# Sampled rows' input projection of the gated DeltaNet layer: column halves side by side, three weight slots, output rows ahead of the scan's loads

## What is computed

```
def _dn_branch(xn, S0, conv_buf, w_in, conv_w, A_log, dt_bias, o_gain, w_out):
    qkv, z, b, a = _split(xn @ w_in, (3072, 1024, 8, 8))
    qkv, new_buf = _short_conv(qkv, conv_buf, conv_w)      # silu of a 4-tap convolution; new_buf: last 3 rows of each request
    ...                                                    # q, k normed; delta rule over chunks of rows
    beta = sigmoid(b)
    g = -exp(A_log) * softplus(a + dt_bias)
    o, S_new = _gated_delta_chunked(q, k, v, g, beta, S0)
    return (_rms_norm(o, o_gain) * silu(z)) @ w_out, S_new, new_buf
```

## Time and profile before

| what | value |
|---|---|
| median of three runs | 2249.23 us (2243.47 to 2261.52) |
| the profiled execution's own time | 2251.16 us |
| its span, first to last instruction | 2248.6 us |
| around the span | 2.6 us |
| TensorE busy, mean granted clock | 90% of the span, 0.948 |
| `dn_sample`, from its first TensorE transpose to the scan's first | 1686.4 to 1763.1 us, 76.7 us |

### The profile page before, as it was taken

One profiled execution on the slowest core, in us unless ns is written; L12 is line 12 of the kernel. 1 busy time (PEld: TensorE's weight loads), 2 busy tenths in 40 slices (PEclk: granted clock), 3 DMA queues, 4 the chain that ended last, 5 costly groups with the idle time before them and its releaser, 6 DMA issues. The chain is left out here.

```text
span 2248.6 us, 25250 instructions
## 1 busy us (share of the span) xinstructions
PE 2030.2 (90%) x9247; PEld 1230.7 (55%) x9247; DVE 1380.2 (61%) x2311; ACT 674.4 (30%) x1699; POOL 502.5 (22%) x544
## 2 busy tenths in 40 slices
PE   6999999998788989788899978989999799999998
PEld 5544344443455566444444545656543687767774
DVE  2478678999678999388683212122332576666662
ACT  3447622121324233111012221112111444443431
POOL 2112100000000000011105666664401512322220
PEclk9999999999999999898999988889999899999999
DMA  4025420110521120212123434343458352233210
GB/s 132 12 77 203 138 87 24 47 47 24 196 78 55 38 85 22 75 42 72 51 56 104 125 113 122 106 120 101 136 189 289 90 180 79 65 82 79 74 45 29
DMA packets 158113, 207.32 MB, mean 92 GB/s; under 512 B 43968, under 2 KB 107768, under 8 KB 157944
## 3 DMA queue, kind: packets, MB, share of 16 engines
q1 hardware_dynamic: 135016, 152.87, 21.1%
q0 software_dynamic: 16896, 50.35, 7.0%
q10 hardware_dynamic: 6080, 2.49, 0.4%
HBM read 161.94 MB, written 43.74 MB: 91 GB/s over the span
## 5 line engine op out<-in xcount | busy, mean ns | idle before, releaser
L1837 PE MATMUL acc_ch<-xnT,w_ch 128*128 128x512 f32 x736 | 367.0, 650 | 5.4 <-ACT x_pad L1870 5.4
L1837 PEld LDWEIGHTS acc_ch<-xnT,w_ch 128*128 128x128 f32 x736 | 147.2, 209 | 168.2 <-issue 163.9
L857 PE MATMUL acc<-w_qg,xnT 128*128 128x512 f32 x384 | 173.5, 606 | 11.5 <-DVE sgate L1011 11.5
L1727 POOL DMA_INDIRECT kg<-in_cache_k,rowidx x128 | 128.2, 1002 | 178.5 <-DVE rowidx L1994 78.4
L1734 POOL DMA_INDIRECT home<-in_cache_v,rowidx x128 | 131.5, 1027 | 64.8 <-issue 31.7
L1052 DVE MAX8 top_v<-scores 128x8 f32<-128x4100 f32 x32 | 141.7, 4430 | 0.7
L1054 DVE FIND_INDEX8 top_i<-top_v,scores 128x8 uint32<-128x4100 f32 x32 | 141.5, 4423 | 0.0
L1056 DVE MATCH_REPLACE8 scores<-top_v,scores 128x4100 f32<-128x4100 f32 x32 | 141.2, 4414 | 0.0
L2799 PE MATMUL PB<-home,ogT_dn 128*128 128x512 f32 x288 | 129.1, 602 | 11.4 <-DVE rhs L3063 10.6
L857 PEld LDWEIGHTS acc<-w_qg,xnT 128*128 128x128 f32 x384 | 72.6, 194 | 96.4 <-issue 84.1
L1233 PE MATMUL ring<-w_out_att,ogT_blk 128*128 128x512 f32 x256 | 114.5, 606 | 4.4 <-DMA w_out_att<-in_att_w_out 2.9
(11 more groups left out here) (437 smaller groups left out, 3719.5 us busy)
## 6 DMA issues: line engine op xcount, KB each, us to landing
home<-in_dn_w_in SPq DMA_DIRECT2D x7, 2048.0 KB, 8.2
w_ch<-in_dn_w_in SPq DMA_DIRECT2D x24, 512.0 KB
qkv_d<-y_ch SPq DMA_DIRECT2D x24, 512.0 KB
qkv_t<-qkv_d SPq DMA_DIRECT2D x8, 1536.0 KB, 7.9
x<-in_x_all SPq DMA_DIRECT2D x9, 512.0 KB, 3.4
out_y_all<-y_t SPq DMA_DIRECT2D x9, 512.0 KB, 2.7
w_z_s<-in_dn_w_in SPq DMA_DIRECT2D x1, 4160.0 KB
w_kvq<-in_att_w_in SPq DMA_DIRECT2D x2, 2048.0 KB, 8.0
```

What stands on the lines that cost most here:

```text
L857: ins = pe.matmul(acc[rows(n), k % ACC, :], xnT[:, kk, cols(n)], w[:, kk, :], start=(kk == 0), stop=(kk == KT - 1))
L1727: pool.indirect_dma_start(kg[:, j % KR, :], None, ck, bass.IndirectOffsetOnAxis(ap=rowidx[:, u % 2, t * QT + u // 2:t * QT + u // 2 + 1], ...
L1837: ins = pe.matmul(acc[:, s, :], w[:, c % WR, k, :], xT[:, k, s * 512:(s + 1) * 512], start=(k == 0), stop=(k == KT - 1))
```

## The change

It touches `dn_sample` alone.

- `project` puts the two halves of 256 columns of a piece side by side: half h goes to output partitions 64h to 64h+63 of the same PSUM bank, two matmuls of 256 columns in place of one of 512 for each k. `gates` does so with the two halves of z (512 columns each). b and a have a load (`w_ba`, 128 x 8 runs of 64 bytes) and matmuls (`steps`) of their own.
- A piece is then 128 partitions x 256 columns: `row` takes it with all 128 partitions (the row scales are copied to partitions 64 to 127 by one more VectorE instruction), and `turn` needs two transposes of 128 x 128 in place of four of 64 x 128. tanh of z is one instruction of 128 x 512 and moves behind the Ln.
- Weight pieces have three slots (`home` twice and `w_more`). Piece 2 is issued at once, piece n from 3 after the matmuls of piece n - 3.
- The old convolution rows have a tile of their own (`cb_n`), so that their load waits for nothing, and their transposes come after the second piece.
- In the queue `wz` comes after the weight pieces, and the stores of the new convolution rows (16 of them now, each 3 rows x 6 runs of 1 KB) come after the constants and ahead of the scan's tile, states, `gz_t1` and `y_t1`.

```
 @block.sync
+            def load(u):
+                if u >= WS:
+                    sp.wait_ge(mm, u - WS + 1)
+                sp.dma_start(w[u % WS], wv[:, :, u * 512:(u + 1) * 512]).then_inc(w_in[u % WS], 16)
-            sp.wait_ge(ss_ok, 1)
             sp.dma_start(cb_n, ...)
+            load(2)
             ...
-            sp.dma_start(wz[:], wv[:, :, CONV:CONV + 1040]).then_inc(wz_in, 16)
-            for n in range(2, CONV // 512):
-                sp.wait_ge(mm, n - 1)
-                sp.dma_start(w[:, n % 2, :, :], wv[:, :, n * 512:(n + 1) * 512]).then_inc(w_in[n % 2], 16)
+            sp.dma_start(w_ba[:], wv[:, :, CONV + DM:CONV + DM + 16]).then_inc(wb_in, 16)
+            for u in range(3, NR):
+                load(u)
+            sp.dma_start(wz[:], wv[:, :, CONV:CONV + DM]).then_inc(wz_in, 16)
             ...                                            # eight constants
+            sp.wait_ge(row_ok, NR)
+            for b in range(DB):
+                for h in range(2):
+                    t = h * NS + (b + 1) * DS
+                    sp.dma_start(d["newbuf_s"][b * 3:(b + 1) * 3, :].rearrange("i (n h j) -> h i n j", h=2, j=HW)[h],
+                                 nat[t - 3:t, :].rearrange("i (n j) -> i n j", j=HW)).then_inc(nb_out, 16)
             sp.dma_start(keep["qkv_t1"][:], ...)
             ...                                            # states, gz_t1, y_t1
-            sp.wait_ge(row_ok, NR)
-            for b in range(DB):
-                sp.dma_start(d["newbuf_s"][b * 3:(b + 1) * 3, :], nat[(b + 1) * DS - 3:(b + 1) * DS, :]).then_inc(nb_out, 16)
-            sp.wait_ge(nb_out, 16 * DB)
+            sp.wait_ge(nb_out, 32 * DB)

 @block.tensor, project(u)
-                    ins = pe.matmul(acc[0:NS, u % 2, :], xT[:, k, :], w[:, u % 2, k, :], start=(k == 0), stop=(k == KT - 1))
+                    for h in range(2):
+                        ins = pe.matmul(acc[h * NS:(h + 1) * NS, u % 2, 0:HW], xT[:, k, :], w[u % WS][:, k, h * HW:(h + 1) * HW],
+                                        start=(k == 0), stop=(k == KT - 1))
 @block.tensor, turn(u)
-                for c in range(4 * u, 4 * u + 4):
-                    ins = pe.transpose(cbp[:, u // 2 % 2, (c % CG) * NS:(c % CG + 1) * NS], nat[:, c * P:(c + 1) * P], ident[0:NS, 0:NS])
+                for i in range(2):
+                    ins = pe.transpose(dst[:, i], nat[:, u * HW + i * P:u * HW + (i + 1) * P], ident[:])
 @block.tensor, gates()
+                    for h in range(2):
+                        ins = pe.matmul(yp[h * NS:(h + 1) * NS, 0, :], xT[:, k, :], wz[:, k, h * 512:(h + 1) * 512], start=(k == 0), stop=(k == KT - 1))
 @block.tensor, order
             for u in range(NR):
                 project(u)
+                if u == 1:
+                    buffers()
                 if u >= 1:
                     turn(u - 1)
-            gates(2)
+            steps()
             turn(NR - 1)
-            gates(0)
-            gates(1)
+            gates()
 @block.scalar
-            for c in range(2):
-                act.wait_ge(z_done, c + 2)
-                act.activation(th[0:NS, c * 512:(c + 1) * 512], yp[0:NS, c, :], ACT.Tanh, scale=rsh[:]).then_inc(th_ok, 1)
             act.wait_ge(ach, 1)
             act.activation(t2[:], t2[:], ACT.Ln, bias=1.0).then_inc(ga, 1)
+            act.wait_ge(z_done, 2)
+            act.activation(th2[:], yp[:, 0, :], ACT.Tanh, scale=rsh[:]).then_inc(th_ok, 1)
 @block.vector
+            dve.tensor_copy(rs[NS:, :], rs[0:NS, :]).then_inc(rs_ok, 1)
```

More of the change, by code:

```diff
@@ L2113, in dn_sample @@
     NR = CONV // 512
-    CH = [(CONV, 512), (CONV + 512, 512), (CONV + 1024, 16)]
     with ExitStack() as ctx:
@@ L2120, in sem @@
             return new_sem(nc, env, "sm_" + name)
-        wz = sb("w_z_s", [P, KT, 1040])
-        w = keep["home"][:].rearrange("p (a k n) -> p a k n", a=2, k=KT)
+        HW = 256
+        WS = 3
+        wz = sb("w_z_s", [P, KT, DM])
+        w_ba = sb("w_ba_s", [P, KT, 16])
+        w_more = sb("w_more_s", [P, KT, 512])
+        home = keep["home"][:].rearrange("p (a k n) -> p a k n", a=2, k=KT)
+        w = [home[:, 0], home[:, 1], w_more[:]]
         x, th = keep["y_t0"], keep["gz_t0"]
+        th2 = sb("tanh_pair", [P, 512])
         go = sb("gain_o_s", [NS, HD])
@@ L2127, in dn_sample @@
         ss = sb("ss_s", [NS, 1])
-        rs = sb("rs_s", [NS, 1])
+        rs = sb("rs_s", [P, 1])
         mhalf = sb("mhalf_s", [NS, 1])
@@ L2138, in dn_sample @@
         thc = sb("tanh_s", [P, NCH, NS])
-        nat = sb("rows_s", [NS, CONV])
-        cb_n, junk = nat[0:NB3, :], nat[:, 0:DM]
+        nat = sb("rows_s", [P, NR * HW])
+        cb_n = sb("conv_buf_s", [NB3, CONV])
+        junk = th[0:NS, :]
         yp = keep["acc_ch"]
@@ L2148, in dn_sample @@
         once = sem("once")
-        wz_in, cb_in = sem("wz_in"), sem("cb_in")
-        w_in = [env["stores"]["ws_in0"], env["stores"]["ws_in1"]]
-        rsh = sb("rs_half_s", [NS, 1])
+        wz_in, cb_in, wb_in = sem("wz_in"), sem("cb_in"), sem("wb_in")
+        w_in = [env["stores"]["ws_in0"], env["stores"]["ws_in1"], sem("ws_in2")]
+        rsh = sb("rs_half_s", [P, 1])
         ss_ok, rs_ok, go_ok, tp_done, xT_ok = (sem(s) for s in ("ss_ok", "rs_ok", "go_ok", "tp_done", "xT_ok"))
@@ L2162, in _ @@
         def _(sp):
-            sp.wait_ge(ss_ok, 1)
-            sp.dma_start(cb_n, d["state_dn_conv"].rearrange("b l i n -> (b l i) n")).then_inc(cb_in, 16)
+            def load(u):
+                if u >= WS:
+                    sp.wait_ge(mm, u - WS + 1)
+                sp.dma_start(w[u % WS], wv[:, :, u * 512:(u + 1) * 512]).then_inc(w_in[u % WS], 16)
+            sp.dma_start(cb_n[:], d["state_dn_conv"].rearrange("b l i n -> (b l i) n")).then_inc(cb_in, 16)
+            load(2)
             sp.dma_start(go[:], d["dn_o_gain"][0:1, :].partition_broadcast(NS)).then_inc(once, 16)
@@ L2195, in _ @@
             link(pool.tensor_scalar(ss[:], ss[:], 1.0 / DM, EPS, ALU.mult, ALU.add))
-            pool.tensor_tensor(rs[:], ss[:], mhalf[:], ALU.pow).then_inc(rs_ok, 1)
-            pool.wait_ge(rs_ok, 1)
+            pool.tensor_tensor(rs[0:NS, :], ss[:], mhalf[:], ALU.pow).then_inc(rs_ok, 1)
+            pool.wait_ge(rs_ok, 2)
             pool.tensor_scalar(rsh[:], rs[:], 0.5, None, ALU.mult).then_inc(rs_ok, 1)
@@ L2217, in _, with buffers @@
             ins.then_inc(tp_done, 1)
[L2218 to L2222, removed]
+            def buffers():
+                pe.wait_ge(cb_in, 16)
+                for c in range(NCH):
+                    ins = pe.transpose(cbp[:, c // 16, (c % 16) * NB3:(c % 16 + 1) * NB3], cb_n[:, c * P:(c + 1) * P], ident[0:NB3, 0:NB3])
+                ins.then_inc(cb_done, 1)
             def project(u):
-                pe.wait_ge(w_in[u % 2], 16 * (u // 2 + 1))
+                pe.wait_ge(w_in[u % WS], 16 * (u // WS + 1))
                 if u >= 2:
@@ L2236, in turn, with steps, gates @@
                     pe.wait_ge(x_ok, 1)
-                for c in range(4 * u, 4 * u + 4):
-                    ins = pe.transpose(cbp[:, u // 2 % 2, (c % CG) * NS:(c % CG + 1) * NS], nat[:, c * P:(c + 1) * P], ident[0:NS, 0:NS])
+                dst = cbp[:, u // 2 % 2, u % 2 * 256:(u % 2 + 1) * 256].rearrange("p (h i t) -> p i h t", h=2, i=2)
+                for i in range(2):
+                    ins = pe.transpose(dst[:, i], nat[:, u * HW + i * P:u * HW + (i + 1) * P], ident[:])
                 if u % 2 == 1:
                     ins.then_inc(tr_done, 1)
[L2242 to L2246, removed]
+            def steps():
+                pe.wait_ge(wb_in, 16)
                 for k in range(KT):
-                    ins = pe.matmul(dst, xT[:, k, :], wz[:, k, a - CONV:a - CONV + n], start=(k == 0), stop=(k == KT - 1))
+                    ins = pe.matmul(bps[0:NS, 0:16], xT[:, k, :], w_ba[:, k, :], start=(k == 0), stop=(k == KT - 1))
                 ins.then_inc(z_done, 1)
+            def gates():
+                pe.wait_ge(wz_in, 16)
+                for k in range(KT):
+                    for h in range(2):
+                        ins = pe.matmul(yp[h * NS:(h + 1) * NS, 0, :], xT[:, k, :], wz[:, k, h * 512:(h + 1) * 512], start=(k == 0), stop=(k == KT - 1))
+                ins.then_inc(z_done, 1)
+            pe.wait_ge(xT_ok, 1)
             for u in range(NR):
                 project(u)
+                if u == 1:
+                    buffers()
                 if u >= 1:
                     turn(u - 1)
-            gates(2)
+            steps()
             turn(NR - 1)
-            gates(0)
-            gates(1)
+            gates()
         @block.scalar
@@ L2261, in _, with buffers @@
             act.activation(junk, x[0:NS, :], ACT.Square, accum_out=ss[:]).then_inc(ss_ok, 1)
[L2262 to L2267, removed]
+            act.wait_ge(rs_ok, 3)
+            def buffers():
+                act.wait_ge(cb_done, 1)
+                for u in range(2):
```

(17 more changed lines are left out.)

## The result

| | before | changed |
|---|---|---|
| median, us | 2250.82 (20 runs) | 2238.73 (20 runs, 2226.13 to 2245.31) |
| ratio of changed to before | | 0.9941, 95% interval [0.9924, 0.9959] |
| span of the profiled execution | 2248.6 | 2231.5 |
| `dn_sample`, first transpose to the scan's first | 1686.41 to 1763.06: 76.65 | 1680.06 to 1746.10: 66.04 |
| from there to the span's end | 485.5 | 485.4 |

12.1 us faster by the medians; by the ratio it is 0.6%. The prediction had 14.7. In the stage itself the gain is 10.6 us; behind it nothing came or went. So I compare stage lengths from here on: identical code gave 66.0 and 66.2.

The account below looks back on a forecast made before the run. A loop of load and matmuls bounds the stage's first half, DMA bytes the second. Terms 28.7 + 10.3 + 10.3 + 4.1 = 53.4 us start the scan 14.7 us earlier: 2249.2 - 14.7 = 2234.5 us, range 2221 to 2249.

Parts of the forecast that it names:

- The block ends with the DMA queue: End of `dn_sample`: SyncE is through issuing at 1747.9, the scan starts at 1748.4 in place of 1763.06.
- The rival in which the queue doesn't hold the block: Issues of states and `gz_t1` return early, z's path ends the block: 26 us less, 2223 us; chance 0.10.
- Pairs: Weight pieces in `project`: paired matmuls of 256 columns overlap, 0.215 us a pair, 3.4 us a piece.
- no overlap: Pairs of 256 columns don't overlap, the last piece ends about 1736: gain 2 us, 2247 us; chance 0.05.
- a low clock: TensorE's clock stays low, pieces take 6.9 us: gain 2 at worst, 8 in the middle, 2241 us; chance 0.08.
- Start of the stream: Weight queue in `dn_sample`: piece 0 ends at 1694.4, piece 3 is issued at 1694.5; b's and a's load costs 0.
- The output rows' price: Stores of new convolution rows: 4.1 us on three engines; their 5.4 us of issues lie beside z's load.
- The sum: From piece 3's issue to the end of `y_t1`'s issue: 28.7, 10.3, 10.3 and 4.1, together 53.4 us.
- output rows nearly free: Stores of new convolution rows cost 0.7 us, spread over all engines: 18.1 us less, 2231 us; chance 0.12.
- The slower rival: Scan's loads queue behind 288 store runs on three engines; priced by runs these cost 49 us: 2280 us; chance 0.03.
- z's path: z's weights land at 1723.2, matmuls take 9.5 us, all done at 1736.6, 11 us before SyncE is through.
- Loads behind the stores: Part of the slower rival, chance 0.03: the scan's loads, 4 MB of states included, queue behind the stores' 288 runs.

Follow-up runs that it names:

- run 6: Changed kernel with the loads of both state halves, `gz_t1` and `y_t1` moved to the scan's queue: stage 52.2 us against 66.04, ratio to before 0.9900.
- run 5: Changed kernel with the two halves of z's matmuls one after the other instead of in pairs: stage 66.2 us against 66.04.
- run 1: Changed kernel with the two halves of a weight piece one after the other instead of in pairs: stage 78.3 us against 66.04.
- run 4: Changed kernel with each of the 16 stores split in two, 3 rows x 3 runs: stage 64.1 us against 66.04.
- run 10: Kernel before the change with its eight stores moved ahead of the scan's loads: stage 82.6 us against 76.65.
- run 9: Changed kernel with two weight slots instead of three: stage 74.6 us against 66.04.
- run 2: Changed kernel with its 16 stores put back behind the scan's loads: stage 73.1 us against 66.04.
- run 8: Kernel before the change with the loads of both state halves, `gz_t1` and `y_t1` moved to the scan's queue: stage 75.8 us against 76.65, ratio 0.9983.

## Why the prediction was right, and what was off

- *The block ends with the DMA queue, after the change with the issues of states and `gz_t1`.* Right, and shown by run 6 (13.8 us when these alone are moved) and run 5 (nothing when TensorE is slowed at the end). The rival in which the queue doesn't hold the block falls.
- *Pairs.* 3.67 us a piece for 3.4; they overlap at 256 columns, and the clock was 1.00 from 1690 to 1705.5, so the rivals of no overlap and of a low clock fall too. Run 1 shows what the pairs are worth here: 12 us, and only by releasing the stores and the scan's loads.
- *Start of the stream.* Piece 3 was issued 7.97 us into the stage, forecast 8.1. But what I wrote beside it, that b's and a's runs of 64 bytes are free because the queue waits for piece 0 anyway, was wrong in kind: the stretch 1688 to 1690 runs at 190 GB/s and a share of 1.04, at piece 3's issue, so the DMA engines were not waiting. Two us at 190 in place of some 385 GB/s are about 1 us of the stream. In runs 5 and 6 piece 3 was issued 0.4 us earlier and the last constant's issue came no earlier for it (32.2 us into the stage each time). That the 64-byte runs are the cause is argued from these rows; a run without the load wasn't made.
- *The output rows' price* is the step that was mis-sized. The prediction let the issues of the 16 stores (0.34 us each, 5.4 in all) lie beside z's load and charged only 4.1 us of bytes on three engines. The bytes were sized well (68 GB/s in run 4 for the 72 assumed), but a store took SyncE 0.78 us from one issue to the next, 12.5 in all. Of these 6.5 lay behind the last of the weights and constants, and the data of the scan's tile began to move 1.5 us after the last of them: together the hole of 8 us. So it is SyncE's issuing that costs and not the three engines. The sign that the prediction named for this, a share of 0.17 for much over 4 us, is there.
- *The sum.* The stream, 53.4 us from piece 3's issue to the end of `y_t1`'s, was 57.6. Of the 4.2 between them 1.3 lie ahead of z's landing (30.0 us after piece 3's issue, where the sum has 28.7), the 64-byte runs most likely; 2.9 lie behind it, where the hole was 3.9 longer than the term and about 1 was made up, which I have not traced. That the gain in the stage is 10.6, to the digit that of the upper bound of 8.2 us for the stores, is therefore luck.
- *The other prices of the rows.* The rival "output rows nearly free" falls. The slower rival had the right kind of price for part of it, by the run and not by the byte, with a chance of 0.03. It put it on the three engines, where the runs of run 4 passed at 68 GB/s, about 45 ns each on an engine; SyncE's issues come to 12.5 us, where 18.8 would have decided against the change.
- *z's path.* Forecast 50.2 us into the stage (1736.6), measured 50.6, by two misses that cancel: the weights landed 1.1 us later, and the matmuls took 8.48 us in place of 9.5.
- *Loads behind the stores.* This part of the slower rival is real: in the kernel before it costs 6 us (run 10), in the changed one it is what makes run 1 slower than before. What kept it from deciding is that the last piece ends 31 us into the stage, where it was 54 before.

So the parts depend on each other: three slots (8.6 us, run 9), pairs (12, run 1) and the order of the queue (7, run 2) are each worth two thirds of the gain of 10.6 or more, their sum is far more than the gain, and run 10 shows one of them alone as a loss.

## What to carry to other kernels

Where a block ends with a DMA queue, ask what the queue's own engine must still issue. Behind other transfers each of the states' and `gz_t1`'s loads held SyncE for 3.5 to 8.0 us, and loads that nobody in this block needs were better issued at the head of the next one (14 us here, more than any single part of the change is worth). Before moving small stores ahead of something, look at how long their issues take and not only at their bytes: the same output rows took SyncE 12.5 us as 16 DMAs of 3 rows and 4.1 as 6 of 8 rows. And judge a reordering in the kernel in which it will stand: moving the stores ahead is a loss of 6 us with late data (eight stores, run 10) and a gain of 7 with early data (sixteen, run 2).

## What the runs showed of the hardware that I had not expected

- The issue of a small store of 1 KB runs takes SyncE as long beside full DMA engines as beside idle ones: 0.72 us for 3 rows x 6 runs, 0.28 for 3 x 3, 0.61 for 8 x 6. Three engines, fed by such issues, move 25 GB/s; with stores piled up, 68.
- A load of half the states took SyncE 0.84 us to issue after a pause of 5.8 us in the queue (run 6), and 3.62 in the changed kernel, right behind the tile's.
- Two 256-column matmuls one after the other on the same half of the columns: 32 in 6.32 us, 0.20 each, less than half of the 0.43 between two of 512.
- Eight stores of 12 KB rows took 2.70 us to issue behind the scan's loads, but 4.93 in run 10 and 4.91 in run 8, where the queue had run empty ahead of them. One issue of 1.6 us is over half of the difference; why it takes so long stays open.
